# Gate product of a streaming encoder layer as seven products over the two halves of each block, on one Trainium2 core

## Chip, cores and metric

One core of one Trainium2 chip. The metric is the device time of one execution in microseconds; the median of three executions before the change was 2050.23 us (2049.8 to 2053.08).

## The reference

One layer on x of 4096 tokens by 1024 channels, in fp32. What the change touches is the end of it, from the output projection on:

```python
n = _rmsnorm(h, norm_w[i])
z = n @ w_in[i]                       # projections, gated linear attention, short conv: not touched
...
h = h + jnp.concatenate([y_gla, y_conv], axis=-1) @ w_out[i]      # 1024 x 1024

gate = jax.nn.sigmoid(h @ w_ple_gate[i] + b_ple_gate[i])          # 1024 x 1024: the gate product
h = h + gate * (p[i] @ w_ple[i])                                  # p: 256 wide
...
return _rmsnorm(h, final_norm_w)
```

## The kernel before

Channels lie on the 128 partitions, tokens along the free axis, in 8 blocks of 512 tokens (TB). Each fp32 product is made of three matmuls in fp32r: an operand is split into a high part (a rounding copy, on ACT or POOL) and a low part (the difference, on DVE or POOL), and high x high, low x high and high x low are added in PSUM.

There are four phases in a row, the same on every engine's program. The first (`gla`, 8 blocks) projects, normalises and runs the attention; meanwhile POOL prepares weights for later (`prep_pair`, 12 pairs of tiles) and writes them to w_scratch in DRAM. Then come 12 steps of seven products each: 8 `conv` steps and, from `CONV_STEPS` = 8 to 11, the 4 output steps (`out_proj`), which compute h. A step takes two blocks of 512 tokens as the two columns of a 2 x 2 scheme (quadrants Q11, Q12, Q21, Q22: half of the channels by block) and forms seven products P1, P6, P7, P2, P5, P3, P4 (in this order) in place of eight; their operands need differences of quadrants (t3 = Q22 - Q12 and t1 on POOL in `difference`, t2 and t4 on DVE in `make_t2`, `make_t4`), and their results are added on ACT (copies of PSUM to EA, EB) and DVE (`add_copies`, `add_products`, L1860 and L1872). A product has 4 output tiles x 4 input tiles x 3 matmuls of 512 columns, a step 336 matmuls. Its weights (2 MB for each of the seven) are combinations of weight tiles: that is what `prep_pair` makes.

Every engine works its queue strictly in order. On POOL a step is: t3 of this step, a wait for P6's split, t1 (once t4 is made), then the loads of the next step's quadrants Q12, Q11, Q22, Q21, each behind the split that frees its place. DVE makes t2 of step g+1 ahead of the additions of step g's P4, and these free the PSUM banks of the next P1. The additions of P2 come behind P5's split, and free the banks of P5. In the slots that `GATE_SLOTS` names (steps 8, 9, 10) POOL also splits ten tiles (two of W_ple, eight of W_gate) into g_scratch (`prep_tile`, L712 and L715).

The last phase is the gate stage, `gate(b)` for 8 blocks. For each of 8 output tiles PE makes the W_ple product (6 matmuls, L1150 to L1152) and the gate product (`big_tile`, 24 matmuls of 512 columns, L814, L815, L822), ACT the sigmoid (L1474), DVE gate x ple and the sum into h (L1935, L1937), ACT the square (L1481), DVE their sum (L1922). In the next block's second tile PE forms the mean by a matmul with ones (`out_stats`), ACT the root, DVE the reciprocal and `final_norm`; SP stores the block and loads the one after next. The gate weights all lie in SBUF (WP, WG), loaded in step 11 by `next_weights` as its products give up their weights.

## Time and profile before

| | us |
|---|---|
| median of three runs | 2050.23 |
| profiled execution, its own time | 2053.48 |
| span of its records | 2051.7 |
| PE busy | 2001.9 |
| DVE busy | 1387.2 |
| ACT busy | 738.3 |
| POOL busy | 578.8 |
| output steps (1280 to 1600), PE busy | 314.2 of 320 |
| gate stage (1600 to 2040), PE busy | 436.8 of 440 |

The times of instructions come from the one profiled execution; its span is from the first to the last recorded instruction. A matmul's shown length (0.39 us with 512 columns) is longer than the distance to the next, since they are pipelined: distances are read from the starts. PEld is the weight load, which overlaps PE. A releaser in square brackets names who ended an engine's idle time.

### The profile page before, as it was taken

Reading aid. Unit: us, or ns where it says so; the run is one execution under the profiler, and the core shown is the slowest. Engines: PE = TensorE matmul, PEld = TensorE weight load, DVE = VectorE, ACT = ScalarE, POOL = GpSimd, SP = SyncE. Lnnn points to the kernel's source line nnn. Section 1 sums busy time; section 2 is a strip of 40 time slices with the busy share of each in tenths; the row PEclk is TensorE's granted clock in tenths of the full one; section 3 lists DMA queues with packets and bytes.
Section 4 is the critical chain, followed back from the end, with each engine's and each line's share of the span. In section 5 each row is a group of like instructions: output and inputs, shape, how many; then the busy total and the mean of one; then the engine's idle time right before and its main releaser. Section 6 shows DMA issues by size and latency. Waiting matters only on the chain.

```text
span 2051.7 us, 25908 instructions
## 1 busy us (share of the span) xinstructions
PE 2001.9 (98%) x9730; PEld 1664.6 (81%) x9730; DVE 1387.2 (68%) x1554; ACT 738.3 (36%) x1106; POOL 578.8 (28%) x590
## 2 busy tenths in 40 slices
PE   6999999999999999999999999999999999999997
PEld 5888788888888888888888888878887888888885
DVE  6888888879875776576577577557555456565654
ACT  5444454545534432322332332322322233333331
POOL 4765666766651112112112112254411000000000
PEclk9999999999999999999999999999999999999998
DMA  6355355354445412127212137676677322222111
GB/s 233 118 180 195 124 192 197 133 199 162 171 164 242 158 62 88 57 103 292 97 62 88 57 121 277 207 284 241 218 237 275 110 93 93 92 92 83 66 76 41
DMA packets 82390, 306.72 MB, mean 149 GB/s; under 512 B 10064, under 2 KB 18688, under 8 KB 71808
## 3 DMA queue, kind: packets, MB, share of 16 engines
q1 hardware_dynamic: 53152, 179.17, 24.1%
q0 software_dynamic: 29152, 126.40, 16.9%
q8 instruction: 54, 0.88, 0.2%
q14 instruction: 32, 0.26, 0.0%
HBM read 183.90 MB, written 121.63 MB: 149 GB/s over the span
## 4 chain that ended last, share of the span: by engine, by line
PE 84%; DVE 8%; issue 3%; DMA 2%; ACT 1%; POOL 1%; SPq 0%; DVEq 0%; ACTq 0%; POOLq 0%
PE bank L1064 13%; PE bank L1070 13%; PE bank L1066 13%; PE bank L814 12%; PE bank L822 12%; PE bank L815 12%; PE bank L1152 1%; PE bank L1151 1%; PE bank L1150 1%; DVE raw L1554 1%; PE bank L899 1%; DVE XL L1529 1%; DVE rt L1570 1%; PE bank L959 1%; DVE hist L1638 1%
## 5 line engine op out<-in xcount | busy, mean ns | idle before, releaser
L1064 PE MATMUL bank<-XH,WC 128*128 128x512 f32 x1344 | 526.3, 392 | 5.9 <-DVE xt L1872 5.8
L1070 PE MATMUL bank<-XL,WC 128*128 128x512 f32 x1344 | 524.2, 390 | 0.2 <-DVE XL L1706 0.2
L1066 PE MATMUL bank<-XH,WC 128*128 128x512 f32 x1344 | 524.3, 390 | 0.0
L1706 DVE TENSOR_TENSOR XL<-RQ,XH 128x1024 fp32r<-128x1024 f32 x168 | 210.4, 1288 | 235.3 <-ACT XH L1377 234.4
L1064 PEld LDWEIGHTS bank<-XH,WC 128*128 128x128 f32 x1344 | 252.9, 188 | 60.1 <-DVE xt L1872 7.1
L1070 PEld LDWEIGHTS bank<-XL,WC 128*128 128x128 f32 x1344 | 253.1, 188 | 53.3 <-DVE XL L1706 0.6
L1066 PEld LDWEIGHTS bank<-XH,WC 128*128 128x128 f32 x1344 | 253.2, 188 | 52.0
L752 POOL TENSOR_TENSOR RQ<-RQ 128x1024 f32<-128x1024 f32 x48 | 114.8, 2414 | 428.4 <-DVE RQ L1725 407.4
L1377 ACT ACTIVATE XH<-RQ 128x1024 fp32r<-128x1024 f32 x168 | 170.6, 1053 | 165.6 <-PE bank L1070 138.6
L815 PE MATMUL bank<-XH,WG 128*128 128x512 f32 x512 | 199.3, 389 | 0.0
L814 PE MATMUL bank<-XH,WG 128*128 128x512 f32 x512 | 199.3, 389 | 0.0
L822 PE MATMUL bank<-XL,WG 128*128 128x512 f32 x512 | 199.2, 389 | 0.0
L1935 DVE TENSOR_TENSOR t_sb<-gt,bank 128x512 f32<-128x512 f32 x64 | 43.9, 685 | 186.4 <-ACT gt L1474 186.4
L814 PE MATMUL bank<-XH,QG 128*128 128x512 f32 x384 | 152.4, 397 | 0.0
L822 PE MATMUL bank<-XL,QG 128*128 128x512 f32 x384 | 149.8, 390 | 1.0 <-DVE hist L1638 1.0
L815 PE MATMUL bank<-XH,QG 128*128 128x512 f32 x384 | 149.9, 390 | 0.0
L1394 ACT ACTIVATE EA<-bank 128x512 f32<-128x512 f32 x96 | 57.4, 600 | 184.8 <-PE bank L1070 84.1
L814 PEld LDWEIGHTS bank<-XH,WG 128*128 128x128 f32 x512 | 96.1, 188 | 20.1
L822 PEld LDWEIGHTS bank<-XL,WG 128*128 128x128 f32 x512 | 96.1, 188 | 20.1
L815 PEld LDWEIGHTS bank<-XH,WG 128*128 128x128 f32 x512 | 96.1, 188 | 19.9
L658 POOL TENSOR_TENSOR PB<-PB,prep_hi 128x512 f32<-128x512 f32 x84 | 109.3, 1301 | 2.3
L1570 DVE RECIPROCAL rt<-rt 128x512 f32<-128x512 f32 x32 | 107.0, 3344 | 2.6 <-ACT rt L1271 2.5
(188 smaller groups left out, 3447.0 us busy)
## 6 DMA issues: line engine op xcount, KB each, us to landing
WC<-w_scratch SPq DMA_DIRECT2D x21, 2048.0 KB, 8.5
RQ<-n_scratch POOLq DMA_DIRECT2D x32, 1024.0 KB, 5.4
w_scratch<-prep_hi POOLq DMA_DIRECT2D x84, 256.0 KB, 2.3
w_scratch<-PB POOLq DMA_DIRECT2D x84, 256.0 KB, 2.3
raw<-xb_dram SPq DMA_DIRECT2D x32, 512.0 KB, 5.9
n_scratch<-raw SPq DMA_DIRECT2D x8, 2048.0 KB, 7.1
y_scratch<-y_sb SPq DMA_DIRECT2D x64, 256.0 KB, 2.4
RQ<-y_scratch POOLq DMA_DIRECT2D x16, 1024.0 KB, 6.6
```

The costliest lines, as they stand in the source:

```text
L658: pool.tensor_tensor(PB[:, buf], PB[:, buf], prep_hi[:].bitcast(F32), ALU.subtract).then_inc(prep_done, 1)
L752: pool.tensor_tensor(RQ[:, a, k], RQ[:, Q22, k], RQ[:, b, k], ALU.subtract).then_inc(made, 1)
L814: nc.tensor.matmul(acc_ap, hh[0], hh[1], start=(k == 0), stop=False)
L815: nc.tensor.matmul(acc_ap, lh[0], lh[1], start=False, stop=False)
L822: mm = nc.tensor.matmul(acc_ap, hl[0], hl[1], start=False, stop=(k == KT - 1))
L1064: nc.tensor.matmul(bank[:], WC[:, i, q, 0, k], xh, start=(k == 0 and i in (P1, P2, P5)), stop=False, skip_group_check=True)
L1066: nc.tensor.matmul(bank[:], WC[:, i, q, 1, k], xh, start=False, stop=False, skip_group_check=True)
L1070: mm = nc.tensor.matmul(bank[:], WC[:, i, q, 0, k], xl, start=False, stop=(k == 3), skip_group_check=True)
L1377: nc.scalar.activation(XH[:, slot(s) + 2 * h:slot(s) + 2 * h + 2], RQ[:, OPERAND[i], 2 * h:2 * h + 2], ACT.Copy).then_inc(sx_hi, 1)
L1394: nc.scalar.activation((EB if i == P6 else EA)[:, q], ps[A_BANK[q]][:], ACT.Copy).then_inc(e_copied, 1)
L1570: nc.vector.reciprocal(rt[:], rt[:]).then_inc(head_step, 1)
L1706: nc.vector.tensor_tensor(XL[:, k], RQ[:, OPERAND[s % 7], 2 * h:2 * h + 2], XH[:, k].bitcast(F32), ALU.subtract).then_inc(sx_lo, 1)
```

## The change

The gate product takes the seven-product form too, for each block alone: the two columns of the scheme are the two halves of 256 tokens (HT). A product (`gate_product`) is 4 output tiles x 4 input tiles x 3 matmuls of 256 columns, two output tiles side by side in one PSUM bank; the W_ple product (`ple_unit`) is made for pairs of output tiles and one half, also with 256 columns. The operands t1 to t4, the high parts and the low parts (one instruction of 1024 columns for each product) are made by ACT (`gate_hi`) and DVE (`gate_t3`, `gate_t2`, `gate_t1_t4`, `gate_lo`) from the block in SBUF. P1, P6, P7, P4 go to banks 3 and 4 and are copied out by ACT (`gate_copy`) between them; P2, P5, P3 go to banks 0 and 1, and DVE adds the copies (`gate_sum`, six a block). The sigmoid is done in halves of 256 columns, since a unit holds two output tiles with their own bias; mix and square go by units of two tiles x 256 tokens, eight a block. The mean and the normalisation of block b - 1 lie in block b; the last block is not treated apart any more.

The gate weights are now seven sets of 2 MB, prepared like the others: four pairs more (phase 3 of `w_scratch`), cut in parts `prep_load`, `prep_a`, `prep_b`, `prep_c`, which POOL does in slots of steps 8, 9 and 10 instead of the tiles; the two W_ple tiles are done in step 11 before t1, one after the other. SP loads the seven sets in step 11 and behind the last of them both parts of W_ple, in front of the last four stores of h; it waits for the W_ple tiles (tile_stored) at the start of step 11. `over_blocks` is no longer used for this stage.

```diff
                 sp.wait_ge(sx_free, 4 * (7 * g + i + 1))
-                if g < STEPS - 1:
-                    if i == P1:
-                        wait_prepared(sp, g // NP + 2)
-                    load_weights(g // NP + 1, i)
-                elif i < 5:
-                    tile = WP[:] if i == 0 else WG[:, 2 * i - 2:2 * i]
-                    sp.dma_start(tile.bitcast(F32), g_scratch[i].rearrange("p (m h k c) -> p m h k c", m=2, h=2, k=KT)
-                                 ).then_inc(w_chunk[i], 16)
+                if i == P1:
+                    wait_prepared(sp, g // NP + 2)
+                load_weights(g // NP + 1, i)
...
                         load_xt(n)
                 if g == STEPS - 1:
-                    sp.wait_ge(tile_hi_stored, 16 * GATE_TILES)
-                    for half in range(2):
-                        sp.wait_ge(tile_lo_stored[half], 16 * GATE_TILES // 2)
+                    sp.wait_ge(tile_stored, 16 * 2 * PLE_K)
                     sp.dma_start(p_raw[:], pb[0]).then_inc(p_loaded, 16)
                 next_weights(g, P1)
...
                         sp.wait_ge(h_stored[c], 16 * 2 * (NP - 1))
                     load_raw(raw, h_scratch[0], NB)
                 next_weights(g, P5)
-                for n in range(4, 16):
+                for n in range(4, 8):
+                    store_h(first + n)
+                next_weights(g, P3)
+                for n in range(8, 12):
+                    store_h(first + n)
+                if g == STEPS - 1:
+                    next_weights(g, P4)
+                    for part, tile in enumerate((WPH, WPL)):
+                        sp.dma_start(tile[:].bitcast(F32), g_scratch[part].rearrange("p (k m c) -> p k m c", k=PLE_K, m=KT)
+                                     ).then_inc(wp_loaded, 16)
+                for n in range(12, 16):
                     store_h(first + n)
...
+            def combine(n, ph, made, to, a, b, op):
+                buf = buffers_of(ph)[0]
+                pool.tensor_tensor(buf[:, to], buf[:, a], buf[:, b], op).then_inc(prep_done, 1)
+                pool.wait_ge(prep_done, 18 * n + made + 1)
+            def split(n, ph, q, made, i, j, hi_before):
+                buf, hi = buffers_of(ph)
+                if hi_before > 0:
+                    pool.wait_ge(prep_stored[5], 16 * hi_before)
+                pool.tensor_scalar(hi[:], buf[:, j], 1.0, 0.0, ALU.mult, ALU.add).then_inc(prep_done, 1)
+                pool.wait_ge(prep_done, 18 * n + made + 1)
+                part = slice(2 * q * TB, 2 * q * TB + TB)
+                pool.dma_start(w_scratch[ph, i, :, part], hi[:].bitcast(F32)).then_inc(prep_stored[5], 16)
+                pool.tensor_tensor(buf[:, j], buf[:, j], hi[:].bitcast(F32), ALU.subtract).then_inc(prep_done, 1)
+                pool.wait_ge(prep_done, 18 * n + made + 2)
+                part = slice(2 * q * TB + TB, 2 * q * TB + 2 * TB)
+                pool.dma_start(w_scratch[ph, i, :, part], buf[:, j]).then_inc(prep_stored[j], 16)
...
                     pool.wait_ge(prep_stored[4], 16 * n)
-                combine(4, 2, 3, ALU.add)
-                combine(2, 0, 2, ALU.subtract)
-                split(P7, 2, 7 * n, 0)
-                split(P4, 3, 7 * n + 1, 0)
+                combine(n, ph, 0, 4, 2, 3, ALU.add)
+                combine(n, ph, 1, 2, 0, 2, ALU.subtract)
+                split(n, ph, q, 2, P7, 2, 7 * n)
+                split(n, ph, q, 4, P4, 3, 7 * n + 1)
...
-                combine(2, 4, 0, ALU.subtract)
-                split(P5, 4, 7 * n + 2, 0)
-                split(P1, 0, 7 * n + 3, 0)
+                combine(n, ph, 6, 2, 4, 0, ALU.subtract)
+                split(n, ph, q, 7, P5, 4, 7 * n + 2)
+                split(n, ph, q, 9, P1, 0, 7 * n + 3)
...
-                combine(3, 1, 2, ALU.subtract)
-                split(P2, 1, 7 * n + 4, 0)
-                split(P6, 2, 7 * n + 5, 0)
-                split(P3, 3, 7 * n + 6, 0)
...
-                dst = g_scratch[n // 2, :, half * 2 * D_MODEL:(half + 1) * 2 * D_MODEL]
                 if n == 0:
-                    load_tile(0)
-                load_tile(n + 1)
-                pool.wait_ge(tile_loaded[half], 16 * (n // 2 + 1))
...
-                    pool.wait_ge(tile_hi_stored, 16 * n)
-                pool.tensor_scalar(tile_hi[:], tile_raw[:, half], 1.0, 0.0, ALU.mult, ALU.add).then_inc(tile_split, 1)
+                    wait_prepared(pool, 4)
+                else:
+                    pool.wait_ge(tile_stored, 16 * 2 * n)
...
                 pool.wait_ge(tile_split, 2 * n + 1)
-                pool.dma_start(dst[:, 0:D_MODEL], tile_hi[:].bitcast(F32)).then_inc(tile_hi_stored, 16)
-                pool.tensor_tensor(tile_raw[:, half], tile_raw[:, half], tile_hi[:].bitcast(F32),
-                                   ALU.subtract).then_inc(tile_split, 1)
+                pool.dma_start(g_scratch[0, :, columns], tile_hi[:].bitcast(F32)).then_inc(tile_stored, 16)
...
                 difference(g, Q12, Q12, t3_made)
-                if g in GATE_SLOTS:
-                    prep_tiles(g, 0)
+                if g == CONV_STEPS + 1:
+                    prep_c(3, 0)
+                    prep_load(3, 1)
+                    prep_a(3, 1)
+                elif g == CONV_STEPS + 2:
+                    prep_b(3, 2)
+                    prep_c(3, 2)
+                    prep_load(3, 3)
+                elif g == STEPS - 1:
+                    for n in range(PLE_K):
+                        prep_tile(n)
                 split_waits(s + P6)
-                if g in GATE_SLOTS:
-                    prep_tiles(g, 1)
+                if g == CONV_STEPS + 1:
+                    prep_b(3, 1)
+                elif g == CONV_STEPS + 2:
+                    prep_a(3, 3)
                 pool.wait_ge(t4_made, 2 * (g + 1))
                 difference(g, Q11, Q11, t1_made)
                 if g == STEPS - 1:
...
-                if g in GATE_SLOTS:
-                    prep_tiles(g, 2)
+                if g == CONV_STEPS:
+                    prep_load(3, 0)
+                    prep_a(3, 0)
+                elif g == CONV_STEPS + 1:
+                    prep_c(3, 1)
+                    prep_load(3, 2)
+                elif g == CONV_STEPS + 2:
+                    prep_b(3, 3)
                 split_waits(s + P3)
                 pool.wait_ge(t1_made, 2 * (g + 1))
                 load_quadrant(g + 1, Q22)
+                if g == CONV_STEPS:
+                    prep_b(3, 0)
+                elif g == CONV_STEPS + 1:
+                    prep_a(3, 2)
+                elif g == CONV_STEPS + 2:
+                    prep_c(3, 3)
                 split_waits(s + P4)
                 load_quadrant(g + 1, Q21)
...
+            def gate_product(b, i):
+                z = 7 * b + i
+                banks = GATE_A if i in (P1, P6, P7, P4) else GATE_C
+                for q in range(4):
+                    if b == 0 and q == 0:
+                        pe.wait_ge(w_chunk[i], 16 * 4)
+                    if q % 2 == 0:
+                        wait_gate_bank(b, i, q // 2)
+                    if q == 0:
+                        pe.wait_ge(gx_hi, z + 1)
+                    acc_ap = ps[banks[q // 2]][:, q % 2 * HT:q % 2 * HT + HT]
+                    for k in range(4):
+                        xh, xl = XHg[:, z % 2, k], XLg[:, z % 2, k]
+                        nc.tensor.matmul(acc_ap, WC[:, i, q, 0, k], xh, start=(k == 0 and q % 2 == 0 and i in (P1, P2, P5)),
+                                         stop=False, skip_group_check=True)
+                        nc.tensor.matmul(acc_ap, WC[:, i, q, 1, k], xh, start=False, stop=False,
+                                         skip_group_check=True)
+                        if q == 0 and k == 0:
+                            pe.wait_ge(gx_lo, z + 1)
+                        mm = nc.tensor.matmul(acc_ap, WC[:, i, q, 0, k], xl, start=False, stop=(k == 3),
+                                              skip_group_check=True)
...
+            def wait_gate_bank(b, i, pair):
+                if i in (P1, P2) and b == 0:
+                    wait_out_read((GATE_A if i == P1 else GATE_C)[pair])
+                elif i == P1:
+                    pe.wait_ge(g_sig, 8 * (b - 1) + 7 + pair)
+                elif i == P2:
+                    pe.wait_ge(g_sum, 6 * (b - 1) + 5 + pair)
+                elif i == P6:
+                    pe.wait_ge(g_copied, 6 * b + 1 + pair)
+                elif i == P7:
+                    pe.wait_ge(g_copied, 6 * b + 3 + pair)
+                elif i == P5:
+                    pe.wait_ge(g_sum, 6 * b + 1 + pair)
+                elif i == P3:
+                    pe.wait_ge(g_sum, 6 * b + 3 + pair)
+                else:
+                    pe.wait_ge(g_copied, 6 * b + 5 + pair)
...
+            def gate(b):
+                gate_product(b, P1)
+                gate_product(b, P6)
+                if b > 0:
+                    out_stats(b - 1)
+                gate_product(b, P7)
+                for c, i in enumerate((P2, P5, P3, P4)):
+                    gate_product(b, i)
+                    ple_unit(b, 2 * c)
+                    ple_unit(b, 2 * c + 1)
...
+                    act.wait_ge(g_t2, b + 1)
+                elif i == P7:
+                    act.wait_ge(g_t3, b + 1)
+                elif i == P5:
+                    act.wait_ge(g_t1, b + 1)
+                elif i == P4:
+                    act.wait_ge(g_t4, b + 1)
+                if z < 2:
+                    act.wait_ge(sx_free, 4 * (7 * STEPS - 1))
+                else:
+                    act.wait_ge(g_prod, 4 * (z - 1))
+                nc.scalar.activation(XHg[:, z % 2], gate_operand(z), ACT.Copy).then_inc(gx_hi, 1)
...
+            def gate(b):
+                z = 7 * b
+                gate_hi(z + P6)
+                gate_copy(b, P1, 0)
+                gate_copy(b, P1, 1)
+                gate_hi(z + P7)
+                gate_copy(b, P6, 0)
+                gate_copy(b, P6, 1)
+                gate_hi(z + P2)
+                split_p_hi(b)
+                if b > 0:
+                    out_rms(b - 1)
+                gate_hi(z + P5)
+                sigmoid(b, 0)
+                gate_copy(b, P7, 0)
+                sigmoid(b, 1)
+                gate_copy(b, P7, 1)
+                gate_hi(z + P3)
+                gate_square(b, 0)
+                gate_square(b, 1)
+                sigmoid(b, 2)
+                sigmoid(b, 3)
+                gate_hi(z + P4)
+                gate_square(b, 2)
+                gate_square(b, 3)
+                sigmoid(b, 4)
+                sigmoid(b, 5)
+                gate_hi(z + 7)
+                gate_square(b, 4)
+                gate_square(b, 5)
+                for u in (6, 7):
+                    sigmoid(b, u)
+                for u in (6, 7):
+                    gate_square(b, u)
...
+            def gate_lo(z):
+                if z == 7 * NB:
+                    return
+                dve.wait_ge(gx_hi, z + 1)
+                nc.vector.tensor_tensor(XLg[:, z % 2], gate_operand(z), XHg[:, z % 2].bitcast(F32),
+                                        ALU.subtract).then_inc(gx_lo, 1)
...
+            def gate_sum(b, u):
+                n, pair = 8 * b + u, u % 2
+                if n == 0:
+                    for c in range(8):
+                        dve.wait_ge(h_stored[c], h_count)
+                if n >= 3:
+                    dve.wait_ge(g_mixed, n - 2)
+                dve.wait_ge(g_prod, 4 * (7 * b + (P2, P5, P3)[u // 2]) + 2 * pair + 2)
+                other = EBg if u >= 4 else EAg
+                dve.wait_ge(g_copied, 6 * b + (1, 5, 3)[u // 2] + pair)
+                nc.vector.tensor_tensor(gt[:, n % 3], ps[GATE_C[pair]][:], other[:, pair], ALU.add).then_inc(g_sum, 1)
...
+            def gate_mix(b, u):
+                n = 8 * b + u
+                dve.wait_ge(g_sig, n + 1)
+                dve.wait_ge(ple_done, n + 1)
+                nc.vector.tensor_tensor(gt[:, n % 3], gt[:, n % 3], ps[PLE_BANK[n % 3]][:], ALU.mult).then_inc(
+                    g_scaled, 1)
+                dve.wait_ge(g_scaled, n + 1)
+                here = unit_view(raws[b % 2], u)
+                nc.vector.tensor_tensor(here, here, two(gt[:, n % 3]), ALU.add).then_inc(g_mixed, 1)
...
+            def gate(b):
+                z = 7 * b
+                gate_lo(z + P6)
+                gate_lo(z + P7)
+                gate_t1_t4(b)
+                gate_lo(z + P2)
+                split_p_lo(b)
+                if b > 0:
+                    out_recip(b - 1)
+                    final_norm(b - 1, range(4))
+                gate_lo(z + P5)
+                if b > 0:
+                    final_norm(b - 1, range(4, 8))
+                gate_sum(b, 0)
+                gate_sum(b, 1)
+                gate_lo(z + P3)
+                gate_mix(b, 0)
+                gate_mix(b, 1)
+                gate_sum(b, 2)
+                gate_sum(b, 3)
+                add_square(b, 1)
+                gate_lo(z + P4)
+                gate_mix(b, 2)
+                gate_mix(b, 3)
+                gate_t3(b + 1)
+                gate_sum(b, 4)
+                gate_sum(b, 5)
+                add_square(b, 3)
+                gate_lo(z + 7)
+                gate_mix(b, 4)
+                gate_mix(b, 5)
+                gate_t2(b + 1)
+                add_square(b, 4)
+                add_square(b, 5)
+                gate_mix(b, 6)
+                gate_mix(b, 7)
+                add_square(b, 6)
+                add_square(b, 7)
+                gate_total(b)
```

## Rows read from the trace of the kernel before

**Rows 1.** The page's busy time: us (share of the span) xinstructions.

```profile
PE 2001.9 (98%) x9730; PEld 1664.6 (81%) x9730; DVE 1387.2 (68%) x1554; ACT 738.3 (36%) x1106; POOL 578.8 (28%) x590
```

**Rows 2.** Busy by stretch: us, PE, PEld, DVE, ACT, POOL, clock, DMA, GB/s.

```profile
1280.00:1600.00 320.00, 314.19 (x1370) 258.87 (x1369) 192.63 (x203) 91.02 (x114) 92.41 (x76) 0.99 0.70 243
1600.00:2040.00 440.00, 436.80 (x1921) 360.19 (x1919) 235.56 (x339) 144.29 (x221) 0.00 (x0) 1.00 0.21 76
```

**Rows 3.** Order of time (start, us, engine, ...): PE's narrower matmuls.

```profile
359.80 0.29 PE L814 MATMUL bank<-KAH,XH 128*128 128x272 f32 x1
...
365.35 0.29 PE L822 MATMUL bank<-KAH,XL 128*128 128x272 f32 x1
...
373.21 0.40 PE L936 MATMUL bank<-wup,aT 96*128 96x256 f32 x2
...
347.10 1.05 PE L899 MATMUL bank<-q_diag,hist 128*128 128x128 f32 x8
```

**Rows 4.** Order of time, PE: the output steps' long waits.

```profile
1360.78 0.50 PE L1064 MATMUL bank<-XH,WC 128*128 128x512 f32 x1 [3.10 <-DVE xt L1872]
...
1361.62 0.63 PE L1064 MATMUL bank<-XH,WC 128*128 128x512 f32 x1
...
1572.38 0.50 PE L1064 MATMUL bank<-XH,WC 128*128 128x512 f32 x1 [2.25 <-DVE xt L1872]
```

**Rows 5.** Order of time, POOL's differences (L752) and DVE's additions (L1872).

```profile
1352.33 4.74 POOL L752 TENSOR_TENSOR RQ<-RQ 128x1024 f32<-128x1024 f32 x2 [9.92 <-DMA RQ<-y_scratch]
...
1543.91 5.49 POOL L752 TENSOR_TENSOR RQ<-RQ 128x1024 f32<-128x1024 f32 x2 [40.89 <-DVE RQ L1725]
...
1554.08 1.27 DVE L1872 TENSOR_TENSOR xt<-xt,bank 128x512 f32<-128x512 f32 x2
```

**Rows 6.** Order of time, DVE: splits, additions, a mix (product, then sum).

```profile
1506.49 2.35 DVE L1706 TENSOR_TENSOR XL<-RQ,XH 128x1024 fp32r<-128x1024 f32 x2
...
1589.89 2.47 DVE L1872 TENSOR_TENSOR xt<-xt,bank 128x512 f32<-128x512 f32 x4
...
1818.32 0.68 DVE L1935 TENSOR_TENSOR t_sb<-gt,bank 128x512 f32<-128x512 f32 x1
1819.03 0.69 DVE L1937 TENSOR_TENSOR raw_odd<-raw_odd,t_sb 128x512 f32<-128x512 f32 x1
```

**Rows 7.** ACT in order of time; its sigmoid by form.

```profile
1526.65 0.60 ACT L1394 ACTIVATE EA<-bank 128x512 f32<-128x512 f32 x1 [2.12 <-PE bank L1070]
1527.15 2.00 ACT L1377 ACTIVATE XH<-RQ 128x1024 fp32r<-128x1024 f32 x2
...
L1474 ACT ACTIVATE gt<-bank,vec 128x512 f32<-128x512 f32 x64 | 44.0, 688 | 178.8 <-PE bank L822 178.8
```

**Rows 8.** Order of time: the end of the span.

```profile
2034.41 0.40 PE L822 MATMUL bank<-XL,WG 128*128 128x512 f32 x1
...
2037.72 1.28 ACT L1486 ACT_TABLE_LOAD   x1
...
2039.01 0.69 ACT L1486 ACTIVATE R_out<-bank,eps 128x512 f32<-128x512 f32 x1
...
2043.12 5.39 DVE L1955 SCALAR_TENSOR_TENSOR raw_odd<-raw_odd,vec,R_out 128x512 f32<-128x512 f32 x8
```

**Rows 9.** Order of time, POOL: a weight pair and the next.

```profile
387.74 3.54 POOL L645 TENSOR_TENSOR PB<-PB 128x512 f32<-128x512 f32 x2 [4.43 <-issue]
...
398.85 1.30 POOL L645 TENSOR_TENSOR PB<-PB 128x512 f32<-128x512 f32 x1
...
424.17 0.55 POOL L672 DMA_DIRECT2D PB<-w_out_dram  x1 [2.62 <-DMA w_scratch<-PB]
...
431.98 2.65 POOL L645 TENSOR_TENSOR PB<-PB 128x512 f32<-128x512 f32 x2 [6.71 <-issue]
```

**Rows 10.** DMA issues by line: size of each, median us from issue to landing.

```profile
h_scratch<-xt SPq DMA_DIRECT2D x64, 256.0 KB, 5.2
```

**Rows 11.** Order of time, DVE: four additions beside POOL's work.

```profile
1419.97 11.72 DVE L1860 TENSOR_TENSOR xt<-xt,EB 128x512 f32<-128x512 f32 x4
```

455 lines of the change are left out of this document (256 added, 199 removed).

## Prediction, made before the changed kernel was run

> **What bounds the kernel now.** I read the page's busy table first: PE is busy 2001.9 of 2051.7 us over 9730 matmuls, all other engines far less [rows 1]. Then the busy time by stretch: from 1600 us on (the gate stage) PE has no gap, DVE is busy 235.6 of 440 us and POOL does nothing; in 1280 to 1600 us (the four output steps) PE misses 5.8 us and the clock is below full [rows 2]. Then the starts of single matmuls, because their shown length (389 ns) is longer than their spacing. From 1600 us on 1921 of them fill 436.8 us, so with 512 columns they start 0.227 us apart [rows 2]. So the gate stage is bound by the number and width of its matmuls: 8 blocks of 192 + 48, and 14 for the means, 1934 x 0.227 = 439 us, which is what lies between 1595.9 us and the last of them at 2034.6 us.
>
> The output steps are not quite bound by PE. A step is 336 matmuls, 76.2 us. PE waited for DVE's additions to xt for 3.1 and 2.25 us [rows 4]. The first, at 1357.5 us, hangs on POOL: it had the two W_ple tiles between two of its loads, so Q22 of the next step was issued late and POOL waited 9.9 us for it, its difference began at 1352.33, DVE's make_t2 waits for that in order, and behind make_t2 stand the additions that free PE's banks [rows 4, 5]. After the 3.1 us wait eight matmuls are shown with 0.63 us and start 0.43 apart, the low one of the two clock levels (1.2 instead of 2.4 GHz), 1.7 us more in all [rows 4]. The second wait hangs on an xt load behind 2 MB of weights on SP's queue.
>
> **Gate product: what PE saves.** Removed: 1536 matmuls of 512 columns. Added: 8 x 7 x 48 = 2688 of 256 columns; the 384 of the W_ple product become 768 of 256. The trace has no long run with 256. Two neighbours: 272 columns start 0.126 us apart (44 intervals in 5.55 us), and with 128 columns eight start in 0.78 us, 0.111 apart, where the weight load sets the pace [rows 3]. From 512 to 272 each column costs 0.42 ns, so 256 gives 0.1195 us, above the 0.111 of the weight load; a pair with 256 columns is 0.40 us for two, again 0.12 [rows 3]. A block is then 432 x 0.1195 + 0.45 for the means = 52.1 us against 54.9. If 256 behaved like 272 it were 54.9, no gain; those are the two ends, and I take 0.1195 because two rows meet there. Eight blocks: 22 us at most.
>
> **Gate product: the ring of waits that takes its place.** New on DVE for each block: four differences of operands (t3, t2, t1, t4), six sums, seven splits of 1024 columns where eight of 512 were. New on ACT: six copies out of PSUM, sigmoids in halves of 256 columns. Durations: DVE two inputs of 1024 columns 1.28 us, and 1.1 to the next; of 512 columns 0.69, 0.60 to the next if independent, 0.72 if it waits for its own result; normalisation 0.665 each; reciprocal 3.39; ACT 1024 columns 1.06 (two in 2.00), PSUM copy 0.60 with 0.50 to the next, table load 1.28, root 0.69 [rows 6 to 8]. A sigmoid of 256 columns isn't in the trace: 512 take 0.69, and copies of 1024 against 512 columns (1.06, 0.60) give 0.90 ns a column, so 0.46; a pair 0.75 to 0.94. Each engine's total stays under the block (DVE about 43, ACT about 27). But the queues are in order and call each other. Followed once round a block from DVE's split of P6, which PE's third P6 matmul waits for: rest of P6 5.8 us; ACT copy, split of P2, split of p, table load, root 4.55; DVE reciprocal, four normalisations, split of P5, four more, first sum 10.5 (PE's P5 waits here); ACT two sigmoids with two copies, split of P3 3.6; DVE split, two mixes, two sums, ACT sigmoids, split of P4 7.0; DVE split, two mixes, t3, sum, ACT two sigmoids and the next block's P1 split 8.1; DVE split, two mixes, t2, two additions, two mixes, two additions, the total with its split, and at last P6's split 13.4. Sum 53.0 us. The ring is thus 0.9 us longer than PE's own 52.1, and PE stands still about 0.5 us before P5 and 0.3 in P6. I add 0.3 a block for hand-overs that I set to zero: 53.3. Block 0 has no normalisation before it: 51.7. Stage: 51.7 + 7 x 53.3 = 424.8, 13.9 less than 438.7. Ends for a block: 52.1 (-22 for the stage) and, with every sigmoid pair at 0.94 and each mix at 1.45 us instead of 1.32, about 56 (+5).
>
> **The end.** Before, from the last matmul of the product to the end of the span it is 17.1 us, with the root starting 4.4 us in [rows 8]. After, the last mix, its square, two additions, total, high part and low part (about 4.9 us after PE's end) and two matmuls stand before the root, 5.7 us in: +1.3.
>
> **The start of the stage** costs nothing: DVE's additions of P3's products end at 1592.4 [rows 6], t3, t2 and P1's split follow to 1596.2, and PE needs them at 1596.1. What covers it is P4 of the last step; without that it were 3.8 us. On SP, gate weights P3 and P4 (2 MB each, and W_ple 2 MB) go in front of the last store_h: those land about 18 us into the stage, the first sum needs them (h_stored) at 20, and P5 needs that sum at 26, so 6 us of cover. The second wait of PE, 2.25 us plus its low clock, stays: SP's order around it is the same.
>
> **Weights in parts of pairs: what POOL loses.** Removed from POOL: eight W_gate tiles in steps 8 to 10. Added: four pairs, each 4 combinations and 7 splits. The twelve pairs of the projection phase took 44 us each on POOL: part a 11.1 (387.74 to 398.85), b and c with the store they wait for 25.3 (to 424.17), the load 7.8 until used [rows 9]. By their operations (two, one and one combinations, two, two and three splits) I take a as 10.7, b 9.4, c 13.1, store 2.6, load 7.8. POOL is in order; behind each part stand the loads of the next step's quadrants, t3 (4.75 us) and t1. Two deadlines from the rows: PE goes on 3.7 us after t3's end at a step's start [rows 4, 5], and P5's banks come free 5.4 us after t1's end (1549.4 to 1554.8) [rows 5], so t1 must end 38.2 us into a step.
> Step 8: load and a(0) from 1317.9 to 1337.2, Q22 out 4 us earlier than before, b(0), Q21, t3 of step 9 ends 1352.5: PE doesn't wait at 1357.5, which gives back 3.5 and the low clock's 1.7.
> Step 9: c(0), load, a(1), b(1) are 43.6 us, t1 ends at 1400.9, 43.4 us into the step: PE waits 5.3 before P5. Then c(1), the load of pair 2, Q22, a(2), Q21, t3: ends 1443.2, PE goes on at 1446.9 instead of 1440.8: 6.1 more.
> Step 10: b(2), c(2), load, a(3) are 43.6 again: t1 ends 1491.5, PE waits 4.8 before P5. b(3), c(3), t3 end at 1522.9, in time for step 11.
> Waits 16.2 and, since 2.25 us was enough before, three times the low clock at 1.7 and 0.1 for each restart: 21.6; minus the 5.7 that steps 8 to 10 lose today: step 11 starts 15.9 us later (1531.5 for 1515.5). In step 11 two W_ple tiles hold SP (tile_stored) until some 23 us into the step; behind SP's wait stand p, W P1 and P6, which have 50 us of time.
>
> **Sum:** +15.9 -13.9 +1.3 = +3.3 us on a profiled run of 2053.5 us (span 2051.7 and 1.8 around it). The median of the runs is 2050.2, so I forecast 2053.6.
>
> **Rivals.** (A) POOL keeps up, and it gets faster. A pair loses 10.4 us waiting for its own DMAs; a block row of h landed in 5.2 us in these very steps [rows 10], and the wait for the store may be hidden where a pair's load stands in a later slot. With 5.2 less for each pair t1 ends in time in both steps, t3 of step 10 costs 3.0 + 1.7 and all else stands as today: step 11 starts 0.8 earlier, 2050.2 - 0.8 - 12.6 = 2037. For it: this is a wait, not work. Against: of the 43.6 us in one slot 33.2 are work. (B) POOL gets slower still. DMA share in these steps is 0.70, and 256 KB of h took 5.2 us to land [rows 2, 10]; prep_hi is one buffer, and a split takes it again 2.8 us after the store before was issued. With stores that need 3.8 us the 16 splits up to t3 of step 10 cost 1 us more each, +16 with step 10's: 2068; from 2.8 us on it costs. (C) DVE is held up by POOL. Four additions of 2.5 us took 11.7 while POOL made t3 and split a tile [rows 11]. POOL's two-input work in steps 8 to 10 rises by 33 us; DVE has about 26 us to spare in each step; were a third of it to hit additions that PE waits for, 10 us: 2064. The Trainium skill (SBUF — State Buffer, "SBUF: two separate sides") says that VectorE with two SBUF inputs and GpSimd reading SBUF hold a shared port pair for a whole instruction, the second being fully blocked; by that rule all 33 us could hit. The row agrees in kind: the additions held have two SBUF inputs, xt and EB [rows 11]. (D) The ring is 56 us: +19 on the forecast, 2072. B, C and D all end on the slow side.
>
> **Chances.** Forecast (POOL late three times, ring at 53) 0.45, own range 2046 to 2064; A 0.28; B 0.10; C 0.08; D 0.06; else 0.03. About 0.2% (4 us) is what a measurement of this kernel can tell from no change. Faster: A nearly whole and a seventh of the forecast, 0.32; within: 0.4 of the forecast and little else, 0.21; slower 0.47. Range 2034 to 2072.
>
> **What would show it.** Matmuls with WC in the gate stage 0.12 us apart; in each block PE idle before P5 for a gate_sum and in P6 for DVE's split, 53.3 us from block to block; POOL without idle in steps 9 and 10, and PE idle twice before P5 (about 5 us) and once at the start of step 10 (6 us), each followed by matmuls at the low clock; none at the start of step 9. I am wrong if 256 columns take 0.126 us or more, if POOL's pairs take under 39 us, or if a block takes over 55.

## The result, and the profile after

| | median, us | runs |
|---|---|---|
| kernel before | 2051.65 | 2049.8 to 2053.3 |
| changed kernel | 2084.8 | 2081.6 to 2088.0 |

The change makes the kernel slower: ratio 1.0162, 95% interval 1.0143 to 1.0181. The forecast was 2053.6 us with a range of 2034 to 2072, so the time lies 13 us above the range's end. The profiled execution after spans 2083.4 us, 31.7 more than before. By stages, cut at the first matmul of step 8, at the first of the last stage and at the last matmul with a weight:

| us | before | after | moved | forecast |
|---|---|---|---|---|
| up to step 8 | 1281.2 | 1282.3 | +1.1 | 0 |
| output steps | 314.7 | 350.7 | +36.0 | +15.9 |
| gate stage | 438.7 | 431.5 | -7.2 | -13.9 |
| end | 17.1 | 18.9 | +1.8 | +1.3 |

First the page's busy time after, which answers to [rows 1]:

```profile
PE 1991.6 (96%) x11264; PEld 1724.4 (83%) x11264; DVE 1494.5 (72%) x1613; ACT 794.2 (38%) x1202; POOL 659.7 (32%) x686
```

PE's work has shrunk by 10 us and its span has grown. Next the busy time in two stretches (columns as in [rows 2]: us, PE, PEld, DVE, ACT, POOL, clock, DMA share, GB/s):

```profile
1280.00:1600.00 320.00, 286.49 (x1221) 234.50 (x1220) 182.12 (x170) 79.95 (x100) 169.79 (x172) 0.94 0.63 223
1600.00:2060.00 460.00, 449.99 (x3570) 440.45 (x3569) 343.45 (x422) 207.08 (x326) 0.00 (x0) 1.00 0.31 115
```

PE, which missed 5.8 us of this first stretch before [rows 2], now misses 33.5 us of it, POOL is busy 169.8 us in place of 92.4, and the clock is 0.94. What PE waited for from 1280 us on (engine line <- releaser: us in total, times, longest):

```profile
PE bank L1149 <- DVE xt L2078: 34.1, 5, 13.2
PE bank L1241 <- DVE XLg L2150: 6.0, 7, 2.7
PE bank L934 <- DVE total_lo L2197: 4.9, 1, 4.9
PE bank L1235 <- DVE gt L2164: 2.0, 7, 0.3
PE bank L1149 <- issue: 1.2, 1, 1.2
```

The first row is the loss. In order of time its five waits are these; [rows 4] had one of 3.10 and one of 2.25:

```profile
1365.60 0.79 PE L1149 MATMUL bank<-XH,WC 128*128 128x512 f32 x1 [5.33 <-DVE xt L2078]
1366.19 0.63 PE L1151 MATMUL bank<-XH,WC 128*128 128x512 f32 x1
...
1418.96 0.79 PE L1149 MATMUL bank<-XH,WC 128*128 128x512 f32 x1 [7.00 <-DVE xt L2078]
...
1466.65 0.79 PE L1149 MATMUL bank<-XH,WC 128*128 128x512 f32 x1 [13.24 <-DVE xt L2078]
...
1518.62 0.80 PE L1149 MATMUL bank<-XH,WC 128*128 128x512 f32 x1 [6.60 <-DVE xt L2078]
...
1611.10 0.50 PE L1149 MATMUL bank<-XH,WC 128*128 128x512 f32 x1 [1.96 <-DVE xt L2078]
```

They are the start of step 9, P5 of step 9, the start of step 10, P5 of step 10 and a place in step 11. After each of the first four, 7 to 14 matmuls start 0.43 us apart, the lower clock level; the four stretches together lose about 9 us. DVE is the releaser, but look at what DVE waited for ahead of the longest one, and at what POOL did then:

```profile
1459.89 6.11 DVE L1923 TENSOR_TENSOR RQ<-RQ 128x1024 f32<-128x1024 f32 x2 [14.36 <-POOL RQ L814]
1465.92 1.87 DVE L2078 TENSOR_TENSOR xt<-xt,bank 128x512 f32<-128x512 f32 x3
```

```profile
1438.13 0.55 POOL L734 DMA_DIRECT2D PB_late<-w_gate_dram  x1 [5.35 <-DMA w_scratch<-PB_late]
...
1446.44 2.64 POOL L705 TENSOR_TENSOR PB_late<-PB_late 128x512 f32<-128x512 f32 x2 [6.64 <-issue]
...
1457.50 4.64 POOL L814 TENSOR_TENSOR RQ<-RQ 128x1024 f32<-128x1024 f32 x2
```

DVE stood 14.36 us for POOL's difference t3 (L814), then made t2, and only then the additions that free PE's banks. POOL had begun t3 late, because the parts of a pair stood in front of it. It is the chain of [rows 4, 5], longer.

### The profile page after: what moved, and what is told of

The parts are those of the page before. It is cut to its first block, busy times and chain, and to the rows that moved or that the text cites. A ratio compares the mean times of both kernels' runs of the same rounds, so it can differ in the third digit from the quotient of the medians.

```text
span 2083.4 us, 28858 instructions
## 1 busy us (share of the span) xinstructions
PE 1991.6 (96%) x11264; PEld 1724.4 (83%) x11264; DVE 1494.5 (72%) x1613; ACT 794.2 (38%) x1202; POOL 659.7 (32%) x686
## 4 chain that ended last, share of the span: by engine, by line
PE 70%; DVE 12%; issue 6%; POOL 5%; DMA 4%; ACT 2%; SPq 1%; DVEq 0%; ACTq 0%; POOLq 0%
PE bank L1149 11%; PE bank L1155 11%; PE bank L1151 11%; PE bank L899 7%; PE bank L907 7%; PE bank L900 6%; PE bank L1241 4%; PE bank L1235 4%; PE bank L1237 4%; DMA w_scratch<-hi_late 1%; POOL PB_late L717 1%; PE bank L984 1%; DMA PB_late<-w_gate_dram 1%; DVE raw L1760 1%; POOL hi_late L713 1%
## 5 line engine op out<-in xcount | busy, mean ns | idle before, releaser
L1912 DVE TENSOR_TENSOR XL<-RQ,XH 128x1024 fp32r<-128x1024 f32 x168 | 224.9, 1375 | 249.3 <-ACT XH L1501 248.5
L1241 PE MATMUL bank<-XLg,WC 128*128 128x256 f32 x896 | 255.2, 285 | 6.1 <-DVE XLg L2150 6.0
L1235 PE MATMUL bank<-XHg,WC 128*128 128x256 f32 x896 | 254.8, 284 | 2.0 <-DVE gt L2164 2.0
L1237 PE MATMUL bank<-XHg,WC 128*128 128x256 f32 x896 | 254.2, 284 | 0.0
L814 POOL TENSOR_TENSOR RQ<-RQ 128x1024 f32<-128x1024 f32 x48 | 115.0, 2419 | 370.3 <-DVE RQ L1931 358.7
L1241 PEld LDWEIGHTS bank<-XLg,WC 128*128 128x128 f32 x896 | 172.6, 193 | 7.9 <-DVE XLg L2150 7.9
L1235 PEld LDWEIGHTS bank<-XHg,WC 128*128 128x128 f32 x896 | 172.6, 193 | 3.8 <-DVE gt L2164 3.4
L1237 PEld LDWEIGHTS bank<-XHg,WC 128*128 128x128 f32 x896 | 172.5, 193 | 0.3
L899 PE MATMUL bank<-VH,XH 128*128 128x512 f32 x256 | 103.2, 403 | 0.0
```

What stands on the lines that cost most here:

```text
L899: nc.tensor.matmul(acc_ap, hh[0], hh[1], start=(k == 0), stop=False)
L1235: nc.tensor.matmul(acc_ap, WC[:, i, q, 0, k], xh, start=(k == 0 and q % 2 == 0 and i in (P1, P2, P5)), stop=False, skip_group_check=True)
L1237: nc.tensor.matmul(acc_ap, WC[:, i, q, 1, k], xh, start=False, stop=False, skip_group_check=True)
L1241: mm = nc.tensor.matmul(acc_ap, WC[:, i, q, 0, k], xl, start=False, stop=(k == 3), skip_group_check=True)
L1912: nc.vector.tensor_tensor(XL[:, k], RQ[:, OPERAND[s % 7], 2 * h:2 * h + 2], XH[:, k].bitcast(F32), ALU.subtract).then_inc(sx_lo, 1)
```

## The experiments

Eleven kernels ran. Times of stages, waits and single instructions come from one profiled execution of each kernel. The time of a kernel is the median of its timed runs, and its ratio is to the kernel before, run in the same group (medians 2052.4, 2050.4 and 2051.9 us in the three groups). Intervals are 95%.

**1. The gate products alone.** The preparation of the gate pairs is out, and the gate products read weights already prepared for w_out.

```diff
-                if g == CONV_STEPS + 1:
-                    prep_c(3, 0)
-                    prep_load(3, 1)
-                    prep_a(3, 1)
...
-                load_weights(g // NP + 1, i)
+                load_weights(min(g // NP + 1, 2), i)
```

> The changed kernel with the preparation of the gate weights left out: its seven gate products read the sets already prepared for w_out, so its output is not the reference's, and GpSimd has only the two w_ple tiles in step 11. Theory 1 (the loss in the output steps is GpSimd being late with its differences, because of the parts of the pairs): the waits of TensorE at the starts of steps 9 and 10 and ahead of P5 in both go, the output steps take 306 to 311 us instead of 350.7 (304.9 us of them matmuls), the last stage keeps its 431.5 us and the end its 18.9, and the sum is 1282.3 + 308 + 431.5 + 18.9 = 2041 us, about 10 us below the kernel before. Rival (the loss comes with the larger stores and loads that SyncE issues, or with the changed buffers, not with the pairs): the output steps stay above 335 us and the time above 2068 us.

Measured: 2040.0 us, ratio 0.9942 (0.9925 to 0.9959). The output steps take 307.1 us (1279.4 to 1586.5). All of PE's waits from 1280 us on:

```profile
PE bank L1215 <- DVE XLg L2124: 6.4, 8, 1.5
PE bank L908 <- DVE total_lo L2171: 4.9, 1, 4.9
PE bank L1209 <- DVE gt L2138: 2.0, 7, 0.3
PE bank L1123 <- DVE xt L2052: 1.9, 1, 1.9
```

The four waits are gone; the 1.9 us are the fifth, in step 11. Without the preparation the kernel is 0.6% faster than before, and 43.6 us (350.7 - 307.1) of the output steps belong to the preparation.

**2. The pairs alone.** The kernel before with the parts of the pairs at the places of the change.

```diff
-                if g in GATE_SLOTS:
-                    prep_tiles(g, 0)
+                if g == CONV_STEPS + 1:
+                    prep_c(3, 0)
+                    prep_load(3, 1)
+                    prep_a(3, 1)
...
```

> The kernel before, its last stage untouched, with the parts of the four pairs in steps 8 to 11 in place of its eight w_gate tiles; the last stage multiplies by copies of one prepared set, so its output is not the reference's. Theory 1 (GpSimd late with its differences): the output steps carry the whole loss without any gate product, with waits of 5, 7, 13 and 7 us at the start of step 9, ahead of its P5, at the start of step 10 and ahead of its P5; 2051.7 + 36 = 2088 us, 2083 to 2091. Rival (the loss needs the new stage too, through its buffers or its loads): within 5 us of the kernel before, 2052 to 2057 us.

Measured: 2091.3 us, ratio 1.0188 (1.0171 to 1.0205), just above the expected range. PE waits for additions to xt at the same five places, 5.36, 6.83, 10.45, 6.04 and 2.09 us, and a sixth time for 0.36. The loss needs nothing of the new stage.

**3. What the pairs' time is made of.** Three kernels leave out more and more of the late pairs: the stores of the high parts, all stores, and the arithmetic too.

```diff
-                pool.dma_start(w_scratch[ph, i, :, part], hi[:].bitcast(F32)).then_inc(prep_stored[5], 16)
+                if ph < 3:
+                    pool.dma_start(w_scratch[ph, i, :, part], hi[:].bitcast(F32)).then_inc(prep_stored[5], 16)
...
-                if hi_before > 0:
+                if hi_before > 0 and ph < 3:
```

> The changed kernel with the 28 stores of the high parts left out, and with them the waits of each split for the one high buffer; the 28 stores of the low parts, their waits, the loads and the arithmetic stay. The gate products read the sets prepared for w_out, so the output is not the reference's. Theory 2a (every microsecond of GpSimd counts alike, whether it waits for a landing or issues): of the 61 us that leaving out all stores freed, 18.2 us of waits and 28 x 0.59 us of issuing go, 34.7 us, so 35/61 of its gain of 28.2 us in the output steps: they take 334.5 us and the kernel about 2068 us, 2063 to 2073. Rival (the stores of the low parts, on which the combinations and the next load wait, carry the loss): 2077 us or more.

> The changed kernel with the 56 stores of the four late pairs left out, and with them every wait for such a store; the arithmetic and the loads stay. The gate products read the sets prepared for w_out, so the output is not the reference's. Theory 2 (the excess of the parts over the forecast is what the stores cost GpSimd: 28 us of waits for them to land and 56 x 0.59 us of issuing, 61 us over four pairs): the four large waits of TensorE go, the output steps take 312 to 320 us and the kernel 2046 to 2054 us. Rival (arithmetic that runs longer here than in the projection phase, and loads that take 10 us, carry the excess): the waits at the start of step 10 and ahead of its P5 stay above 4 us each, and the time is 2062 us or more.

> The changed kernel with the arithmetic and the stores of the four late pairs left out: only their eight loads of 512 KB stay on GpSimd's queue, with the waits for them. The gate products read the sets prepared for w_out, so the output is not the reference's. It divides the 15.4 us by which the output steps of the kernel without stores (322.5 us) are above those with no pairs at all (307.1 us). Theory 2b (GpSimd's arithmetic, stretched beside VectorE, is what is left): output steps 307 to 311 us, kernel 2039 to 2044 us. Rival (the loads, 8 to 10 us each from issue to landing in the two slots ahead of the loads of the quadrants, and what they take from the transfers of xt): output steps 315 us or more, 2048 us or more.

Measured, beside the two ends:

| late pairs | output steps, us | median of the kernel, us | ratio |
|---|---|---|---|
| whole (the change) | 350.7 | 2084.8 | 1.0162 |
| no stores of high parts | 327.0 | 2061.1 | 1.0055 (1.0035 to 1.0075) |
| no stores | 322.5 | 2056.5 | 1.0017 (1.0006 to 1.0027) |
| loads alone | 308.8 | 2039.0 | 0.9938 (0.9918 to 0.9957) |
| nothing | 307.1 | 2040.0 | 0.9942 |

Taken off in this order, the 28 stores of high parts are worth 23.7 us, the 28 of low parts 4.5, the arithmetic 13.7, the loads 1.7. (In another order the shares could differ: a wait costs PE something only beyond what was slack.) These shares come from one execution each. By the ratios of the timed runs they are 22, 8, 16 and -1 us, each known to about 5 us: the stores of the high parts and the arithmetic are clear, the loads can't be told from nothing. For the first kernel I expected 334.5 us, because I let each microsecond of POOL count alike, and it was 327.0: neither my number nor the rival's. For the second, 322.5 us lies above the expected 312 to 320 and below what the rival asked for (2062 us or more, waits above 4 us at the start of step 10 and ahead of its P5): waits of 3.6 and 3.3 us are left at the starts of steps 9 and 10, and none ahead of a P5. The third went as expected. What the high parts' stores do is in POOL's waits of the changed kernel, 1310 to 1600 us:

```profile
POOL PB_late L705 <- issue: 20.0, 3, 9.3
POOL hi_late L713 <- DMA w_scratch<-hi_late: 18.2, 7, 4.1
POOL w_scratch L716 <- POOL hi_late L713: 10.6, 28, 0.5
POOL w_scratch L720 <- POOL PB_late L717: 10.2, 28, 0.5
POOL PB_late L734 <- DMA w_scratch<-PB_late: 10.0, 3, 5.4
```

There is one buffer hi_late, and a split takes it again some 3 us after the store before was issued. Most stores land in 2.4 us (the median), but seven were later, up to 6.9, and held POOL 2.6 us each on average. Beside these 18.2 us stand 28 x 0.59 us of issuing. Which of the two matters more was not told apart, nor what the transfers of these stores take from the others: a second buffer for the high part was not tried.

The arithmetic's share has a part that isn't POOL's. The same additions of DVE from 1310 to 1590 us, first without late pairs, then without stores (groups by shape: busy us, mean ns, idle before):

```profile
L2040 DVE TENSOR_TENSOR xt<-xt,EB 128x512 f32<-128x512 f32 x16 | 24.0, 1551 | 11.3 <-DMA xt<-xb_dram 11.3
L2040 DVE TENSOR_TENSOR xt<-xt,EA 128x512 f32<-128x512 f32 x32 | 20.1, 685 | 4.8 <-DMA xt<-xb_dram 4.8
```

```profile
L2082 DVE TENSOR_TENSOR xt<-xt,bank 128x512 f32<-128x512 f32 x56 | 35.7, 679 | 15.0 <-PE bank L1159 15.0
L2070 DVE TENSOR_TENSOR xt<-xt,EB 128x512 f32<-128x512 f32 x14 | 31.9, 2332 | 0.0
L2070 DVE TENSOR_TENSOR xt<-xt,EA 128x512 f32<-128x512 f32 x32 | 28.0, 932 | 5.0 <-DMA xt<-xb_dram 5.0
```

EA and EB lie in SBUF like xt. The 32 additions of EA average 685 ns without pairs, 824 in the kernel before (whose POOL splits tiles), 929 in the change and 932 without stores. Those of EB average 1551, 1560, 890 and 2332 ns: it depends on what POOL does just then, and even without late pairs one took 5.65 us. An addition with an input from a bank stays at 678 to 680 in all four. DVE's busy time in the output steps is 173 us without pairs, 188 before, 195 in the change and 203 without stores. The Trainium skill (SBUF — State Buffer, "SBUF: two separate sides") says that VectorE reading two SBUF inputs and GpSimd reading SBUF exclude each other for whole instructions; by that rule the bank additions are free and the others not, and the trace agrees.

**4. One pair per step.** Nothing left out; pair 0 goes to the end of the projection phase, where POOL idled 49.1 us, and pairs 1 to 3 get a step each.

```diff
             load_quadrant(0, Q12)
+            prep_load(3, 0)
+            prep_a(3, 0)
+            prep_b(3, 0)
+            prep_c(3, 0)
             pool.wait_ge(kdec, 2 * NB)
...
+                if CONV_STEPS < g < STEPS - 1:
+                    prep_load(3, g - CONV_STEPS + 1)
+                    prep_a(3, g - CONV_STEPS + 1)
...
+                if g >= CONV_STEPS:
+                    prep_b(3, g - CONV_STEPS + 1)
```

> The whole computation, with the parts of the pairs moved: pair 0 is prepared at the end of the projection phase, where GpSimd idles 49 us before it may load the last quadrants, and pairs 1 to 3 one per output step (load and a ahead of the difference t1, b after the load of Q11, c after the load of Q22). Theory 1 with the measured parts (load 10, a 12, b 14, c 13 us: 25 us in a gap of 39 us ahead of t1, 14 in a slot of 13, 13 in 25 us of slack ahead of t3): no wait of TensorE above 2 us in steps 9 and 10, output steps 308 to 314 us; the first step of the convolution may start 0 to 4 us later. 1282 + 2 + 311 + 431.5 + 18.9 = 2045 us, 2040 to 2051. Rival (a pair does not fit into an output step wherever its parts stand): waits of 3 to 7 us ahead of P5 or at the starts of steps 9, 10 and 11, each with low clock behind it, 2057 us or more.

Measured: 2048.2 us, ratio 0.9991 (0.9971 to 1.0011). The output steps take 310.7 us (1286.6 to 1597.3) and no wait in steps 9 and 10 is above 2 us. The preparation itself hasn't become cheaper: seven of its 21 splits there still wait for their stores, 12.6 us together. It stands where POOL has slack. The price is at the other end: step 8 starts 5.4 us later than in the kernel before, where a delay of 0 to 4 was expected. POOL waits 11.15 us for pair 0's last store before it may load over its buffers, and PE waits in the first step of the convolution.

**5. The start of the gate stage.** DVE's order in step 11 alone.

```diff
+                if g == STEPS - 1:
+                    gate_t3(0)
+                    gate_t2(0)
                 add_copies(g, 2, EB, 4)
+                if g == STEPS - 1:
+                    gate_lo(0)
                 add_products(g, 2, P3)
```

> The changed kernel with VectorE's order changed in step 11 alone: the differences t3 and t2 of block 0 stand ahead of the additions of EB for P3, and the split of the first operand ahead of the additions of P3's products. Theory 3 (the 5.1 us that block 0 takes above the forecast are the wait of its first P1 for that split, 2.73 us, and the low clock behind it, about 2.1 us; and the split waits because VectorE stands in front of two loads of xt that land behind the weights): the wait and the low clock go, block 0 takes 52 us instead of 56.8, and the time falls by 4.8 us, 2084.8 to 2080 us. Rival (the loads of raw for block 0, or the weights of P1, land no earlier than xt): the wait stays within 1 us of 2.7, now for the load, and the time within 1 us.

Measured: 2081.2 us, ratio 1.0157 (1.0139 to 1.0175) against 1.0162. The wait of P1 is gone and one of 2.46 us stands ahead of P6, behind it the rest of the additions and their loads:

```profile
1633.19 0.69 DVE L2078 TENSOR_TENSOR xt<-xt,bank 128x512 f32<-128x512 f32 x1 [5.62 <-DMA xt<-xb_dram]
1634.85 0.69 DVE L2078 TENSOR_TENSOR xt<-xt,bank 128x512 f32<-128x512 f32 x1 [0.97 <-DMA xt<-xb_dram]
1635.46 1.22 DVE L2152 TENSOR_TENSOR XLg<-TB__106,XHg 128x1024 fp32r<-128x1024 f32 x1
```

The cause was right and the cure half: in the profile the stage gained 2.1 us where 4.8 were expected; the intervals of the timed runs are too wide to tell 2 us from none.

**6. The ring of the gate stage.**

```diff
                 gate_lo(z + P6)
+                if b > 0:
+                    gate_total(b - 1)
                 gate_lo(z + P7)
```

> The changed kernel with the sum of squares and its split (total, 2.0 to 2.5 us of VectorE) moved from ahead of the split of P6 of the next block to behind it. Theory 4 (blocks 1 to 7 are set by the ring P4 - sigmoid - mix - squares - total - split of P6 - P6, which is 0.55 us a block longer than TensorE's own work at P6, and by 0.28 us at P5): the wait of 0.55 us ahead of XLg in P6 goes from all seven blocks, the period falls from 53.6 to 53.1 us and the last stage by 3.5 to 4 us, 2084.8 to 2081 us; the 0.28 us ahead of P5 stays. Rival (VectorE's total time in a block is the bound, not the order): the waits move behind P6, to P7 or P5, and the period stays at 53.6 us.

Measured: 2078.9 us, ratio 1.0144 (1.0127 to 1.0161). In blocks 1 to 7 the wait for XLg is gone from all seven and PE has only this one left:

```profile
PE bank L1235 <- DVE gt L2164: 1.9, 7, 0.3
```

The period falls from 53.64 to 52.83 us, where 53.1 was expected; 0.55 of the 0.81 us is the wait, the rest isn't explained. Seven blocks take 5.2 us less, block 0 takes 1.9 us more (waits of 1.20 and 3.63 us for its first splits), and the stage as a whole falls by 3.2 us where 3.5 to 4 were expected.

**7. All together.** Experiments 4 to 6 in one kernel, and ahead of the convolution the load of Q22 waits for two of the buffers only.

```diff
-            for i in range(6):
+            for i in (4, 5):
                 pool.wait_ge(prep_stored[i], 16 * 13 * PREP_STORES[i])
             load_quadrant(0, Q22)
+            for i in range(4):
+                pool.wait_ge(prep_stored[i], 16 * 13 * PREP_STORES[i])
```

> The whole computation: pair 0 at the end of the projection phase and one pair in each output step, both orders of VectorE from the two runs above, and ahead of the convolution the load of Q22 waits only for the two buffers that it overwrites (buffer 4 and the high one), that of Q21 for the rest. From the first such kernel (2048.2 us, profiled span 2046.2 us): the convolution starts 2 to 4 us earlier (there GpSimd waited 11.15 us for the last store ahead of both loads), the waits of 1.24 and 1.42 us in P1 and P6 of block 0 go, and 3.5 us of the ring: 2048.2 - 3 - 2.7 - 3.5 = 2039 us, 2035 to 2043, faster than the kernel before (2052.4) by 0.6%. Rival (VectorE has no slack for the new orders once the waits in the output steps are gone): 2045 us or more.

Measured: 2039.7 us, ratio 0.9942 (0.9926 to 0.9959). The profiled execution was the longest of the five, with a span of 2047.8 us, and shows one way to be long: PE waited 9.13 us at the start of the convolution, where a split of pair 0 had waited 8.3 us for its store. The profiled execution of the next kernel, the same in this place, has no wait of PE there. Then P6's split ahead of the last additions too:

```diff
                 else:
+                    gate_lo(P6)
                     add_products(g, 3, P4)
```

> The whole computation, as the version with one pair per output step and both orders (2039.7 us), with the split of P6's operand of block 0 moved ahead of the additions of step 11's P4 products too. Theory 3 (block 0 waits for splits that stand on VectorE behind two loads of xt; with the first one ahead of them, the wait moved to the second, 2.46 to 3.97 us in the three kernels that have the change or the ring): the wait of 3.97 us ahead of P6 of block 0 goes and none takes its place, 2039.7 - 4.0 = 2036 us, 2033 to 2039. Rival (the next thing that stands there, the loads of raw or the weights of P6, is late by as much): the wait changes its name and the time stays at 2039 to 2041 us.

Measured: 2033.9 us, ratio 0.9928 (0.9902 to 0.9954). It is the lowest median, but by the ratios it can't be told from the kernel just above; that its block 0 takes 51.8 us in place of 58.3 is read from the profiles. All waits of PE from 1280 us to the end of its products:

```profile
PE bank L1142 <- DVE xt L2071: 2.8, 2, 1.7
PE bank L1228 <- DVE gt L2160: 1.9, 7, 0.3
PE bank L1142 <- issue: 1.1, 2, 0.7
```

The output steps take 310.0 us and the gate stage 421.6, with no wait at its start. In a last kernel SyncE (SP) also waited for pair 0's stores before it loaded P6's weights.

> The kernel of the run above, with SyncE waiting for all stores of pair 0 between the load of P1's weights of the convolution and that of P6's, so that 12 MB of weights no longer stand beside the last stores. In the profiled run of the version before, a split of pair 0 waited 8.3 us for its store and TensorE 9.13 us at the start of the convolution. Theory 5 (those stores land late because the seven loads of weights are in flight): GpSimd's waits for stores ahead of Q22 fall from 8 to 11 us to under 4, the convolution starts 3 to 8 us earlier, and the time is 2030 to 2034 us. Rival (the weights of P6 and P7 then come late): a wait of TensorE of 3 us or more in P6 or P7 of step 0, and 2036 us or more.

Measured: 2034.6 us, ratio 0.9914 (0.9891 to 0.9936), the same as without. Its longest wait of POOL for a store ahead of the convolution, where under 4 us were expected and the kernel without SyncE's wait had 4.5:

```profile
POOL RQ L804 <- DMA w_scratch<-prep_hi: 7.8, 1, 7.8
```

The wait did not fall, so the theory is wrong: the loads of P6 and later aren't what holds these stores here. What does stays open.

## Why the prediction was wrong, point by point

**256 columns: right.** Forecast 0.1195 us apart. After:

```profile
1759.76 0.28 PE L1235 MATMUL bank<-XHg,WC 128*128 128x256 f32 x1
...
1765.76 0.28 PE L1241 MATMUL bank<-XLg,WC 128*128 128x256 f32 x1
1765.88 0.28 PE L1235 MATMUL bank<-XHg,WC 128*128 128x256 f32 x1
```

From 1759.76 to 1765.88 us they follow each other 0.12 us apart, as worked out from [rows 3].

**The ring: right.** Forecast 53.3 us a block, 53.0 by the ring. Measured, in PE's order:

```profile
1749.38 0.39 PE L1241 MATMUL bank<-XLg,WC 128*128 128x256 f32 x1 [0.55 <-DVE XLg L2150]
...
1803.01 0.39 PE L1241 MATMUL bank<-XLg,WC 128*128 128x256 f32 x1 [0.55 <-DVE XLg L2150]
```

53.63 us, with waits at the two places named, the sizes the other way round: 0.55 in P6 and 0.28 before P5. Experiment 6 confirms the last leg of the ring; the other legs were not measured one by one. Without its two waits a block takes 52.8 us where 52.1 had been forecast, so that the sum comes so near owes something to the 0.3 us added for hand-overs. Blocks 1 to 7 together took 374.9 us for 373.1.

**"The start of the stage costs nothing": wrong, 4.9 us.** Block 0 took 56.6 us for 51.7. The step that failed here is the time at which DVE ends P3's additions, which I took over from [rows 6] as 3.6 us before PE needs it. After, it was 0.5 us before, because two xt loads that had landed 7.9 and 6.6 us ahead of the stage now landed 6.3 and 3.5 ahead:

```profile
1626.74 0.69 DVE L2066 TENSOR_TENSOR xt<-xt,EB 128x512 f32<-128x512 f32 x1 [10.42 <-DMA xt<-xb_dram]
1629.46 0.69 DVE L2066 TENSOR_TENSOR xt<-xt,EB 128x512 f32<-128x512 f32 x1 [2.03 <-DMA xt<-xb_dram]
```

PE waited 2.73 us and then ran 3.3 us at the lower level. The cover that I named, P4 of the last step, had no room for a landing that varies by 3 us. The late output steps are not the cause: the six other kernels with the new stage and this order of DVE wait there as well, 1.9 to 4.8 us in all, the one without any late pair 3.1. Experiments 5 and 7 show the cause: with one split ahead of those additions the wait moves to the next, with both ahead the waits are gone.

**The end: nearly right.** +1.8 us for +1.3; PE waited the forecast 4.9 us for the last total.

**The parts of the pairs: wrong, and the step that decided.** I sized part a at 10.7, b at 9.4, c at 13.1 and the load until used at 7.8 us, with 2.6 us a pair for its own stores, and from them ended t3 of step 9 at 1352.5 us and let step 9 start without a wait. The rows of pair 0 in step 8, POOL in order of time:

```profile
1329.37 3.76 POOL L705 TENSOR_TENSOR PB_late<-PB_late 128x512 f32<-128x512 f32 x2 [9.27 <-issue]
...
1341.66 1.30 POOL L705 TENSOR_TENSOR PB_late<-PB_late 128x512 f32<-128x512 f32 x1
1343.05 1.48 POOL L713 TENSOR_SCALAR hi_late<-PB_late 128x512 fp32r<-128x512 f32 x1
...
1350.98 1.56 POOL L713 TENSOR_SCALAR hi_late<-PB_late 128x512 fp32r<-128x512 f32 x1 [3.36 <-DMA w_scratch<-hi_late]
...
1356.36 4.73 POOL L814 TENSOR_TENSOR RQ<-RQ 128x1024 f32<-128x1024 f32 x2
1361.04 1.26 POOL L705 TENSOR_TENSOR PB_late<-PB_late 128x512 f32<-128x512 f32 x1
```

The load took 10.3 us (issued at 1319.0), a 11.7, b 14.1: 8.2 us more than 27.9, and t3 ended at 1361.1. In b, 3.36 us are a wait for the high part stored just before and 1.8 are the two copies to hi_late, which took 1.5 us each where the median is 0.64. From there the queue was late for good. Part c, with three splits in a row, was missed most: 18.0, 17.3, 15.6 and 18.0 us for 13.1. Over the four pairs loads, parts and waits for stores came to 196 us for 172. The term mis-sized most is the wait for the pairs' own stores: 28.2 us (18.2 for high parts inside the parts, 10.0 for low parts ahead of the loads) where I had 7.8, three times 2.6. I had taken it from one pair whose splits wait for no store [rows 9]. The trace of the kernel before shows that others did, in POOL's waits from 60 to 600 us:

```profile
POOL prep_hi L653 <- DMA w_scratch<-prep_hi: 18.7, 9, 4.5
```

Nine of its 84 splits stood 18.7 us for the high buffer, up to 4.5 each, and from load to load the pairs took 41.3 to 48.4 us, 44.6 on average. So late stores were there to be seen; but that average is only 1 us above my 43.6, and the 49 us of a pair in the output steps are not in it.

In the long slots the error was small: c, load, a and b ahead of t1 took 46.2 and 44.7 us for 43.6 in steps 9 and 10. But from the end of t1 of step 9 to the end of t3 of step 10 it was 50.2 us for 42.3, with waits of 4.05 us for a high part's store, 5.35 for a low part's and 6.64 behind the load. So the four waits came out as 5.3, 7.0, 13.2 and 6.6 us for 0, 5.3, 6.1 and 4.8, which is 16.0 more, and the low clock behind them as about 9 us in all for 5.1, nearly 4 more: together the 20 us by which the output steps missed (36.0 for 15.9). Experiments 1 and 3 show that the pairs are the cause, 43.6 us in all, and that the stores of the high parts are the largest share. None of my three signs of being wrong was a pair that takes longer than 44 us.

**The rivals.** B (splits wait for their stores) named the right wait, and its 16 us lie near the 18.2 measured, but that is partly luck: B let every store take 3.8 us, while the median was 2.4, less than the 2.8 from which B counted, and seven late ones made the sum. C (DVE held up by POOL) is there too, with a smaller rise than priced: DVE's busy time in the output steps is 195 us, 7 above the kernel before, since DVE was held up there already. On PE's path it can be read from the four waits: from the end of t3 to PE's next matmul it was 4.5 us twice for 3.7, from the end of t1 7.0 us twice for 5.4, 4.8 us in all; in the second the four additions of EA took 4.07 and 4.08 us for 2.49. I had let each rival replace a part of the forecast on its own, 2068 or 2064 us. They came together with it, because they act on the same late queue; the range, cut at the single rivals, was too narrow upwards. A (POOL keeps up) didn't happen in this order of the parts; experiments 4 and 7 show one in which it does.

The 1.1 us up to step 8 lies ahead of all changed work, and the kernels whose program is the same up to there reach step 8 between 1276.0 and 1282.9 us; I don't explain it.
